# Moving the norm's square root to GpSimd and the first silu of each feed-forward block ahead of a weight round, in a 256-token two-block transformer kernel

## What is computed

```
def rms_norm(x, g):
    y = x * lax.rsqrt(jnp.mean(x * x, axis=-1, keepdims=True) + EPS)
    return y * g

def swiglu(x, w_in, w_out):
    gate, up = jnp.split(x @ w_in, 2, axis=-1)
    return (jax.nn.silu(gate) * up) @ w_out

x = x + 0.5 * swiglu(rms_norm(x, ffn1_norm_g[i]), ffn1_w_in[i], ffn1_w_out[i])
...
q = rms_norm(q, q_norm_g)      # per head, in the attention and memory heads
...
return rmsnorm(h, final_norm_w)
```

## Time and profile before

| | |
|---|---|
| median of 3 runs | 1709.72 us (1709.32 to 1709.91) |
| the profiled execution | 1709.77 us, span 1708.1 us, mean granted TensorE clock 0.985 |
| TensorE busy | 1627.5 us, 95% of the span |
| VectorE, ScalarE, GpSimd busy | 1000.0, 806.1, 128.1 us (59%, 47%, 7%) |
| DMA | 277.71 MB, mean 163 GB/s, 49.4% of 16 engines |

### The profile page before, as it was taken

How to read it: one execution, slowest core, us unless ns; L and a number is a source line. 1 busy time by engine, 2 the same in 40 slices (tenths; PEclk the granted TensorE clock), 3 DMA queues, 4 the chain that set the end, 5 groups by cost and what they waited for, 6 DMA issues and landing times. The chain is left out here.

```text
span 1708.1 us, 23310 instructions
## 1 busy us (share of the span) xinstructions
PE 1627.5 (95%) x9257; PEld 1412.0 (83%) x9257; DVE 1000.0 (59%) x1175; ACT 806.1 (47%) x951; POOL 128.1 (7%) x110
## 2 busy tenths in 40 slices
PE   6899999999999999999988999997889999999997
PEld 6788889987888878888776888896789999978886
DVE  5464456475545545456575454589877756755454
ACT  5444453455444544445555444455445534354443
POOL 1000000010000000000300000035751000000000
PEclk9999999999999999999999999998999999999999
DMA  7465555435555555555224555554324656455552
GB/s 228 148 197 173 199 169 154 142 108 165 181 198 182 172 177 179 191 190 163 92 81 142 173 181 188 172 158 139 98 76 127 219 173 192 158 181 185 197 183 75
DMA packets 222454, 277.71 MB, mean 163 GB/s; under 512 B 9140, under 2 KB 203048, under 8 KB 222376
## 3 DMA queue, kind: packets, MB, share of 16 engines
q1 hardware_dynamic: 222376, 276.62, 49.4%
HBM read 275.53 MB, written 1.05 MB: 162 GB/s over the span
## 5 line engine op out<-in xcount | busy, mean ns | idle before, releaser
L1002 DVE TENSOR_TENSOR w_lo<-w_raw,w_hi 128x2048 fp32r<-128x2048 f32 x260 | 595.4, 2290 | 311.3 <-ACT w_hi L575 311.1
L575 ACT ACTIVATE w_hi<-w_raw 128x2048 fp32r<-128x2048 f32 x260 | 497.0, 1912 | 370.7 <-PE ps L1719 272.7
L1717 PE MATMUL ps<-w_hi,xg_hi 128*128 128x512 f32 x912 | 361.3, 396 | 18.4 <-DVE scr L1088 16.8
L1718 PE MATMUL ps<-w_lo,xg_hi 128*128 128x512 f32 x912 | 358.6, 393 | 0.0
L1719 PE MATMUL ps<-w_hi,xg_lo 128*128 128x512 f32 x912 | 358.6, 393 | 0.0
L1709 PE MATMUL ps<-xg_hi,w_hi 128*128 128x256 f32 x1000 | 290.4, 290 | 6.6 <-DVE xg_lo L1010 4.6
L1710 PE MATMUL ps<-xg_lo,w_hi 128*128 128x256 f32 x1000 | 284.9, 285 | 0.0
L1711 PE MATMUL ps<-xg_hi,w_lo 128*128 128x256 f32 x1000 | 284.7, 285 | 0.0
L1717 PEld LDWEIGHTS ps<-w_hi,xg_hi 128*128 128x128 f32 x912 | 173.7, 190 | 57.8 <-DVE w_lo L1002 18.8
L1717 PE MATMUL ps<-w_hi,y_hi 128*128 128x512 f32 x536 | 215.7, 402 | 3.0 <-DVE y_lo L1386 3.0
L1719 PE MATMUL ps<-w_hi,y_lo 128*128 128x512 f32 x536 | 210.2, 392 | 0.0
(11 more groups left out here) (306 smaller groups left out, 1550.3 us busy)
## 6 DMA issues: line engine op xcount, KB each, us to landing
w_raw<-in_ffn_w_in_dram SPq DMA_DIRECT2D x176, 512.0 KB, 4.5
w_raw<-in_ffn_w_out_dram SPq DMA_DIRECT2D x88, 512.0 KB, 4.2
w_raw<-in_w_in_dram SPq DMA_DIRECT2D x82, 512.0 KB, 4.7
w_raw<-in_a_w_in_dram SPq DMA_DIRECT2D x30, 512.0 KB, 4.6
w_raw<-in_w_gate_dram SPq DMA_DIRECT2D x22, 512.0 KB, 3.7
w_raw<-in_w_up_dram SPq DMA_DIRECT2D x22, 512.0 KB, 4.7
w_raw<-in_w_down_dram SPq DMA_DIRECT2D x22, 512.0 KB, 4.1
w_raw<-in_w_ssd_proj_dram SPq DMA_DIRECT2D x16, 512.0 KB, 4.5
```

The costliest lines, as they stand in the source:

```text
L575: act.activation(w_hi[:, u % RING, :], w_raw[:, u % RING, :], ACT.Copy).then_inc(w_rounded, 1)
L1002: dve.tensor_tensor(w_lo[:, s, :], w_raw[:, s, :], w_hi[:, s, :].bitcast(F32), ALU.subtract).then_inc(w_split, 1)
L1717: pe.matmul(dst, xh, hi, start=start, stop=False, skip_group_check=True)
L1718: pe.matmul(dst, xh, lo, start=False, stop=False, skip_group_check=True)
```

## The change

Four edits:

1. `root` on ScalarE is left out for the token norms, the query norms and mixer B's queries. A new `root` on GpSimd raises v to the power -0.5 in one TENSOR_TENSOR instruction (`neg_half` is a constant of 128x32). VectorE's Newton step stays and waits for GpSimd. The wide roots (keys, A heads, B keys, groups) stay on ScalarE.
2. The table set that a phase needs is loaded at its start, ahead of `round_(u + 1)`.
3. In an FFN the first silu of tile 0 goes ahead of `round_(u + 3)`, that of tile 1 behind it; VectorE does the first two products ahead of `split(u + 3)`.
4. At the end TensorE and VectorE take tile 0's two quarters first, each tile has its own root, ScalarE writes the first half of the width and VectorE the second (gain and root in one instruction), and the output DMAs follow by tile.

```diff
@@ GpSimd
+            pool.memset(neg_half[:, :], -0.5).then_inc(pool_done, pool_("neg_half"))
...
+            def root(name, y, v):
+                pool.wait_ge(pool_done, pool_.at("neg_half"))
+                pool.wait_ge(rs_vec, root_.at(name))
+                pool.tensor_tensor(y, v, neg_half[:, 0:v.shape[1]], ALU.pow).then_inc(rs_pool, 1)
...
             for name, _, _ in PHASES[:-1]:
+                root(f"norm {norm_of[name][0]}", rn_y, rn_v)
                 if name in ("mixa", "mixb", "ssd"):
                     {"mixa": mixa, "mixb": mixb, "ssd": ssd}[name]()
+            for tt in range(2):
+                root(f"final {tt}", rn_y[:, tt:tt + 1], rn_v[:, tt:tt + 1])
@@ ScalarE, ffn
                 u = U[f"ffn{f}"]
+                act.preload_act_table_set(SETS["silu"])
...
-                root(rn_y, rn_v)
-                act.preload_act_table_set(SETS["silu"])
-                act.wait_ge(rs_vec, root_.at(f"norm {n}") + 3)
-                round_(u + 3)
+                rooted(f"norm {n}")
...
-                silu(u, 0)
+                silu(u, 0, 0)
+                round_(u + 3)
+                silu(u, 0, 1)
                 step(u + 2, 1, 1, first=True)
@@ ScalarE, the end
-            for j, (tt, h) in enumerate(QUARTERS):
-                act.wait_ge(x_new, 4 * (n - 2) + j + 1)
-                act.activation(sq_out[...], x[...], ACT.Square, accum_out=ssq[:, j:j + 1]).then_inc(squared, 1)
-            root(rn_y, rn_v)
             for tt in range(2):
-                act.wait_ge(rs_vec, 4 * roots[0])
-                act.wait_ge(vec_done, vec.at(f"x gain {2 + tt}"))
-                act.activation(yout[:, tt, 512:], x_gain[:, tt, 512:], ACT.Identity, scale=rcol[:, tt:tt + 1])
+                for h in range(2):
+                    j = 2 * tt + h
+                    act.wait_ge(x_new, 4 * (n - 2) + j + 1)
+                    act.activation(sq_out[...], x[...], ACT.Square, accum_out=ssq[:, j:j + 1]).then_inc(squared, 1)
+                rooted(f"final {tt}")
+                act.wait_ge(vec_done, vec.at(f"x gain {tt}"))
+                act.activation(yout[:, tt, 0:512], x_gain[:, tt, 0:512], ACT.Identity, scale=rcol[:, tt:tt + 1])
@@ VectorE, root_steps
-                dve.wait_ge(rs_act, 2 * k + 2)
+                if pool:
+                    by_pool[0] += 1
+                    dve.wait_ge(rs_pool, by_pool[0])
+                else:
+                    by_act[0] += 1
+                    dve.wait_ge(rs_act, 2 * by_act[0])
@@ VectorE, ffn
                 token_root(n)
-                split(u + 3)
...
                 product(0)
+                split(u + 3)
@@ VectorE, the end
+            def final_root(tt):
+                c = slice(tt, tt + 1)
+                dve.wait_ge(squared, 2 * n + 2 * tt + 2)
+                dve.tensor_tensor(ssq[:, c], ssq[:, 2 * tt:2 * tt + 1], ssq[:, 2 * tt + 1:2 * tt + 2], ALU.add)
+                root(f"final {tt}", rcol[:, c], ssq[:, c], rn_v[:, c], rn_y[:, c], rn_t[:, c], 1.0 / D, pool=True)
...
+            add(n, factor, NU, 0)
+            add(n, factor, NU, 1)
+            gained(0)
+            final_root(0)
+            add(n, factor, NU, 2)
+            add(n, factor, NU, 3)
+            gained(1)
+            output(0)
+            final_root(1)
+            output(1)
@@ SyncE, the end, and TensorE's last down unit: tile 0's quarters first
```

More of the change, by code:

```diff
@@ L250, in build, with quarters @@
         QUARTERS = ((0, 0), (1, 0), (0, 1), (1, 1))
+        def quarters(n):
+            return QUARTERS if n < len(PHASES) - 1 else ((0, 0), (0, 1), (1, 0), (1, 1))
         def quarter(tt, half):
@@ L512, in mixa @@
                                            channel_multiplier=-1).then_inc(pool_done, pool_(f"A e {h} {j}"))
+                root("A query", m_r, m_v)
                 for j in range(4):
@@ L518, in mixb @@
             def mixb():
+                root("B query", m_r, m_v)
                 for j, (t0, n) in enumerate(B_STEPS):
@@ L525, in mixb @@
                     pool.tensor_tensor(xt, xt, tiles(b_rot[:, j % 2])[:, 0:n], ALU.add).then_inc(pool_done, pool_(f"B x {j}"))
+                root("B queries", b_r[:, :, :].rearrange("p a b -> p (a b)"), b_rvt[:, 0:32])
             def weigh(j):
@@ L603, in norm, with rooted, root @@
                 square(n, 1)
-            def root(y, v):
+            def rooted(name):
+                act.wait_ge(rs_vec, root_.at(name) + 3)
+            def root(y, v, name):
                 k = roots[0]
@@ L645, in step @@
                     round_(g + 3, it)
-                    silu(g, i, it)
+                    for tt in range(2):
+                        silu(g, i, tt, it)
                     round_(g + 4, it)
                     hidden_high(i, p)
-                silu(u, 0)
+                silu(u, 0, 0)
+                round_(u + 3)
+                silu(u, 0, 1)
                 step(u + 2, 1, 1, first=True)
                 if f == 0:
-                    root(KB(48, 4), KB(44, 4))
+                    root(KB(48, 4), KB(44, 4), "keys")
                     act.preload_act_table_set(SETS["silu"])
@@ L1060, in token_root @@
                 dve.wait_ge(squared, 2 * n + 2)
-                root(rcol, ssq[:, 0:2], rn_v, rn_y, rn_t, 1.0 / D, name=f"norm {n}")
+                root(f"norm {n}", rcol, ssq[:, 0:2], rn_v, rn_y, rn_t, 1.0 / D, pool=True)
             def token_row(n):
@@ L1206, in query_root @@
                 dve.wait_ge(pe_done, pe_.at(f"{tag} xsum"))
-                root(m_r, ps[:, STAT, 0:8], m_v, m_r, m_t, 1.0 / M_HD)
+                root(f"{tag} query", m_r, ps[:, STAT, 0:8], m_v, m_r, m_t, 1.0 / M_HD, pool=True)
             def mem_max(tag):
@@ L1767, in d_unit @@
                 pe.wait_ge(w_split, u + 1 + 6 * it)
-                for j, (tt, h) in enumerate(QUARTERS):
+                for j, (tt, h) in enumerate(quarters(norm or 0)):
                     tok = slice(tt * P, tt * P + P)
```

99 lines of the change are left out of this document (46 added, 53 removed).

## The result

The changed kernel takes 1687.33 us (median of 4 runs, 1686.99 to 1688.35), the kernel before beside it 1709.52 us (4 runs, 1705.35 to 1709.91). The ratio is 0.9874, with a 95% interval from 0.9859 to 0.9889: faster by 1.3%. The forecast was 1683.3 us with a range from 1679.5 to 1693.5, so the sign and the range hold, and the gain is 4 us smaller than forecast.

The account below looks back on a forecast made before the run. TensorE, busy 95% of the span, was taken as the bound, with its FFN waits and slow clock behind them: 1709.77 - 16.84 - 9.63 + 0.5 - 0.5 = 1683.3 us, range 1679.5 to 1693.5.

Parts of the forecast that it names:

- The FFN waits, 16.84 us: Start of each FFN: TensorE's five waits for the product L1088 go through edits 1 to 3, gaining 16.84 us.
- The spare time, 1.2 us: ffn1's start: the first product ends at 410.6, TensorE is free at 411.79; the wait returns from P = 1.7 us.
- P: Time of the power on GpSimd: taken as 0.5 us for 1 to 8 columns, 1.0 us for 32.
- The clock, 9.63 us: Stretches behind the waits in ffn0, ffn2, ffn3 and ffn4: TensorE keeps 2.4 GHz without idle time ahead, gaining 9.63 us.
- the rival in which the clock falls all the same: Waits go, but as much time at 1.2 GHz stays or comes up elsewhere: 1692.9 us, chance 0.12.
- the argument from ffn1's row that wait and fall aren't one thing: ffn1's wait is as long as the others, yet its clock didn't fall; counted for the clock falling all the same.
- the sentence that three close times speak against much luck: Slow FFN stretches: three times within 0.6 us of each other speak against much luck from run to run.
- Table loads and the memory norm, 0: Loads at phase starts are hidden, cost 0; the memory norm's root costs nothing up to P = 2.3 us.
- Query norms, +0.5 us: Mixers A and B: 8-column roots cost 0; mixer B's 32 columns take 1.0 us in place of 0.56, so +0.5 us.
- The end, -0.5 us: After the last matmul: last outputs 0.1 us later, but half the megabyte already stored, so -0.5 us net.
- First use of the power: Rival in the memory norm: GpSimd loads code once; 1684.8 us at 3.33 us, 1687.5 at 6; within slow power's 0.12.
- The late unit: Rival: split of u+3 or the next unit's rounding comes 1 us late per FFN: 1688 us, chance 0.04.

Follow-up runs that it names:

- experiment 2: Kernel before with edit 3 only (first silu ahead of the weight round, split behind the first product), roots and table loads on ScalarE, old end: 1682.62 us.
- experiment 3: Changed kernel with edit 3 taken back (weight round ahead of first silu, split ahead of first product), everything else kept: 1709.36 us, ratio 0.9999.
- fourth experiment: Kernel before with only VectorE's half of edit 3, split(u + 3) behind the first product, ScalarE's order as it was: 1690.34 us.
- experiment 8: Changed kernel with mixer B's 32-column root on ScalarE and a 14-column power added ahead of each token norm's power: 1695.88 us.
- experiment 7: Changed kernel with mixer B's 32-column root on ScalarE, plus eleven GpSimd products and powers in an idle GpSimd stretch: 1684.84 us, one run.
- experiments 1: Changed kernel with one root, mixer B's 32 columns, back on ScalarE with its table load: 1680.63 us, ratio 0.984.
- experiment 5: Changed kernel with the 8- and 32-column head roots back on ScalarE without table loads of their own: 1680.19 us, ratio 0.9829.
- experiment 6: Changed kernel with 8- and 32-column head roots on ScalarE and the end rearranged, VectorE's last adds during the first power: 1679.51 us, ratio 0.9827.

## Why the prediction was right, and where it fell short

**The FFN waits, 16.84 us: right.** They are gone in all five FFNs. The prediction gave edits 1 to 3 together as the cause, and experiments 2 and 3 take them apart: the order alone gives 1682.62 us and no wait, everything but the order 1709.36. In ffn1 to ffn4 the order is the whole cause; in ffn0 either does nearly all of it (0.39 us of wait are left without the order, none with the order alone). What the prediction didn't say is that, once the order is changed, the root on GpSimd adds nothing at the FFNs. How late silu may come can be read from ffn1 in three experiments, as the start of silu after v and TensorE's wait: in the second 1.79 us and none, in the fourth 3.61 and 1.48 (406.89 against 403.28), in the eighth 4.14 and 2.04 (407.90 against 403.76). Both waits put the limit at 2.1 us. ScalarE's root with its table load is 0.3 us inside it, GpSimd's 0.6.

**The spare time, 1.2 us, and the return from P = 1.7 us: too generous.** In experiment 8 the two powers take 3.3 us together and the wait is 2.04, so it returns from P = 1.3. I had put silu right behind the root and the product right behind silu; the rows show some 0.12 to 0.15 us at three of the hand-overs between engines (v to GpSimd 402.24 to 402.39, silu to product 404.19 to 404.31, and in the fourth experiment product to TensorE 407.93 to 408.08), 0.4 in sum. With P = 0.7 it did no harm.

**The clock, 9.63 us: right in kind and nearly in size.** TensorE's busy time fell by 11.3 us. Waits of 3.0 us and more at this place were followed by half-clock time in 8 of 9 cases (4 of 5 in the kernel before, 4 of 4 in experiment 3), waits of 2.04 us in 2 of 4, waits of 1.5 to 1.8 us in none of 5. That is this place alone: at mixer B's turn of the probabilities the wait is 1.87 to 1.90 us in the kernel before and in all experiments but the third, and half clock stands there in seven of these eight traces (0.70 over 861.57 to 866.00 before), in the eighth experiment not. So the rival in which the clock falls all the same fails, and the argument from ffn1's row that wait and fall aren't one thing was right too. What failed is the sentence that three close times speak against much luck. The kernel before ranges over 5.9 us in 15 runs, and experiment 7 shows 5.4 us of TensorE time with no more idle time. The Trainium skill ("TensorE: Matmul & The Clock Gate", Part 1) calls the number of slow matmuls of one kernel run-variable, and these runs agree. How many of the five stretches fall is in part luck, and 9.63 us is the price of the profiled execution's four. That none falls without the wait isn't luck: the six traces without it (the changed kernel and experiments 1, 2, 5, 6 and 7) have full clock at all 30 FFN starts.

**Table loads and the memory norm, 0: right.** ScalarE's busy time fell by 17.0 us (806.1 to 789.1) and nothing became later. Experiment 2, which keeps the loads, isn't slower. In the memory norm the power took 0.71 us, under the bound given.

**Query norms, +0.5 us: the step that failed.** The term was the price of the power for 32 columns, 1.0 us; it measured 5.44, and the place cost 5.4 us instead of 0.5 (TensorE is 16.4 us ahead of the kernel before at the last matmul in front of it, 841.34 against 857.74, and 11.0 at the turn behind it, 850.55 against 861.57). The working took its bounds from rows of other instructions, of which none is a power (3.33 us for a 128x512 TENSOR_SCALAR as the upper end), and then priced 32 columns at twice the price of two. A fixed part and a part per column would have shown that with only 0.5 us at two columns the slope is open: 32 columns could be anything up to 8 us (0.5 / 2 x 32). Mixer A's query root was entered at 0 on P = 0.5; eight columns took 1.64, and TensorE waits 1.24 us in the attention that follows, which experiment 5 removes.

**The end, -0.5 us: right.** From the last matmul to the end of the span it takes 8.45 us against 8.88, so -0.43. Both halves of the working hold: the last output is written 5.3 us after the last matmul (5.2 before), and the DMAs end 3.1 us behind it (3.7 before). The reading that VectorE's adds stand in one row behind the first root was right, and experiment 6, which takes them out of it among other moves, makes the end 0.7 us shorter.

**First use of the power: not seen.** The first power starts 0.15 us after v (27.71 to 27.86) and took 0.71 us, the others of two columns 0.69 to 0.73. The rival that took a load from the longest GpSimd row fails. The first call into freshly loaded code, for which the Trainium skill ("GPSIMD Engine Reference", 2.1) gives about 6 us, isn't seen at this instruction either.

The terms, in the span: 1708.1 - 16.84 - 9.63 + 5.4 + 1.24 - 0.43 = 1687.8 us, against 1685.3 measured. Here 9.63 is the priced size; busy time fell by 1.7 us more, which is the larger part of the 2.5 us left. 0.8 us, some of it busy time, lie ahead of all roots: TensorE takes the memory norm's root at 29.98 and not at 30.76, and in both kernels that root had long been complete (29.16 and 28.90).

**Rivals.** VectorE does stand behind GpSimd in each root. With P = 0.70 at the token norms it stays covered; the same mechanism decided at the 32 columns, which I had priced in one term only. The late unit didn't come: TensorE's list of waits after has none of L1756, the FFNs' line, for `w_hi` or `w_lo`.

## What to carry to other kernels

- Where an engine in order does a long piece of streaming work (here a round of 1.92 us and a split of 2.29) between a result and its only reader, moving that piece behind the reader can be the whole gain. Try that alone before moving operations to another engine: here it brought 1.5%, and the 32- and 8-column roots moved to GpSimd took a part of it back.
- An instruction without a row has two unknowns, the fixed part and the slope. Price the widest use by itself, and ask what waits for it at that place.
- A wait on TensorE is worth more than its length when slow clock follows it: here halving the waits brought 19 us for 9 us of idle time. Differences under some 5 us between two totals can be clock alone, so read them at places in the trace where both kernels do the same work.

## What the runs showed of the hardware that I had not expected

- GpSimd's power costs 0.39 us and 0.157 us per column of 128 partitions (0.55, 0.70, 1.02, 1.64, 2.90 and 5.4 us for 1, 2, 4, 8, 16 and 32 columns), while its product goes from 0.20 us for 2 columns to 0.25 for 32. ScalarE's logarithm and exponential together take 0.5 us, for 2, 8 and 32 columns alike, as VectorE sees it (waits of 0.50, 0.52 and 0.56 us).
- Equal waits of 2.04 us on TensorE were followed by half clock twice and by full clock twice in one execution. Waits of 1.5 to 1.8 us at the same place were never followed by it (five cases), waits of 1.9 us at mixer B's turn in seven of eight traces.
- TensorE's busy time for the same 9257 matmuls differed by 5.4 us between two kernels that differ in work only at 52 to 76 us, by half-clock stretches beyond 1090 us above all (1619.7 and 1614.3 us). The two ran on different chips; against the fifth experiment, on the same chip, it is 4.2 us.
